# Writing out a layer loop, and moving norms, roundings and transfers ahead, in a two-block network on one core

## The chip, the core and the metric

The kernel runs on one core of a Trainium2 chip. The metric is the device time of one execution in microseconds (us). The core has five engines with queues of their own: PE (TensorE, matmuls), DVE (VectorE), ACT (ScalarE), POOL (GpSimd) and SP (SyncE, which here only starts transfers). They meet through semaphores alone.

## The reference

The input is x, 512 tokens of 1024 features. The first block has two layers. In short:

```
for l in range(2):
    hn = rms_norm(h, g_mix[l]); q, k, v, xr, gr = split(hn @ w_in[l])      # 2560 columns
    q, k = partial_rope(q), partial_rope(k)                                # angles from positions
    lam = exp(sum lam_q0*lam_k0) - exp(sum lam_q1*lam_k1) + lam_init
    o = rms_norm(diff_attention(q, k, v, lam)) * (1 - lam_init)
    y = rg_lru(conv(xr)) * gelu(gr)                                        # rates from softplus(-lru_lambda)
    h = h + concat(o, y) @ w_out[l]
    h = h + square(relu(rms_norm(h) @ w_mlp_in[l])) @ w_mlp_out[l]         # 4096 wide
    h = h + sigmoid(rms_norm(h) @ w_ple_gate[l]) * (p[l] @ w_ple_proj[l])
x = rms_norm(h, g_final)
```

The second block takes that x and a context of 256 tokens, together T = 768. Its first layer is a Mamba-like mixer in 8 head groups: a projection, a convolution, two scans (forwards and backwards), a gate by silu(z), an RMS norm over all 2048 inner features of a token, and an output product; the residual is `h + gate * out`. Its second layer is an attention over the 768 tokens, with 512 outputs, and a last RMS norm. Both layers take scale, shift and gate of every feature from silu(c) @ mod_w. Everything is float32.

## The kernel before

**Layout.** Activations stand with features on partitions: `h` is 128 partitions x 8 blocks x 512 tokens. A sum over features is therefore a matmul with a matrix of ones, and its result is the same row on all 128 partitions.

**Weights.** All large weights are a stream of tiles of 128x2048 floats (1 MB). SP fetches tile n into `wraw` (2 slots). POOL splits it into a rounded part `whi` and a rest `wlo` (2 slots): first four `tensor_scalar`, then four `tensor_tensor`. PE makes three matmuls of each product (whi*hi, wlo*hi, whi*lo), which keeps float32 accuracy. POOL begins tile n+2 when PE has ended tile n (`tile_done`), and PE begins a tile when all of it is split (`wsplit`). A layer has 52 tiles: 10 for `w_in` (`pair(j)`), 4 for `w_out`, 32 for the MLP, 1 for `w_ple_proj`, 4 for the gate and 1 of zeros, which makes the number even, so that the slot is `k % 2` in both passes of the loop. PE doesn't multiply the zero tile; SP fetches it and POOL splits it.

**Inputs of a product.** ACT rounds g*h to `uhi` (one instruction per block of 128 features), DVE writes the rest to `ulo`, PE's first tile of a product waits block by block for `ulo_r`. The norm's factor `rstd` is not in the input: it is applied by DVE when it reads PSUM (`mix_out`, L1544). ACT squares h two blocks at a time, DVE adds the squares into `acc2`, and `norm_sum` makes the sum by a matmul with ones; then come ACT's root and DVE's reciprocal.

**Layers.** `with pe.Fori(0, DEPTH) as l` and the same on ACT and DVE: one body in the program, run twice. At the end of a pass each engine reports, DVE clears all of the layer's semaphores and raises `layer_go`. Then ACT rounds and squares all eight blocks of the finished h for the next layer.

**Opening.** SP starts x and eight small transfers, and then the weights. ACT and DVE wait for all of them (`CST`). DVE makes the rotary angles (L1466 to L1473), ACT their sine and cosine and the tanh for silu(c), and PE waits for all that (`INIT_D`, `INIT_A`).

**Mixer of a layer.** DVE's order behind the first sum: reciprocal, the softplus chain for the LRU's rates (12 small instructions from L2222), `mix_out(0)`, `conv(0)`, `conv(1)`, `mix_out(1)`, `conv(2)`, `conv(3)`, `mix_out(2)`, `mix_out(3)`. ACT: two squares of `gr`, then eight tanhs of the gate products (L452 on PE, L1067 on ACT), which free two PSUM banks by turns.

**Behind the scan.** The last head group ends with eight output blocks on PE, each added by DVE to `oacc` (L1999). Then: `acc` (squares over the features) times ones, a root and a reciprocal over 768 columns (`rs2`); DVE's residual, three instructions per block (L2052, L2054); ACT's squares of it, two blocks at a time; the sum by 16 matmuls, root and reciprocal of 768 columns; and `make_in`, which makes the attention's input block by block (DVE `tin`, ACT scale and shift and `inhi`, DVE `inlo`). PE's first attention tile (K) waits for `inlo` block by block in its first half; its second half follows.

## Time and profile before

| | |
|---|---|
| median of 3 runs | 2680.79 us (2674.96 to 2684.66) |
| the profiled execution | 2680.21 us, span 2678.3 us, mean granted clock 0.965 |
| PE busy | 2442.2 us, 91% of the span |
| DVE, POOL, ACT busy | 54%, 49%, 30% |
| chain that ended last | PE 74%, DVE 15%, issue 5%, ACT 4% |
| HBM read | 194.60 MB, 75 GB/s over the span |

The span runs from the first to the last instruction on an engine. Busy is the time in which an engine has an instruction under way. The chain is followed back from the last instruction, at each step to what released it; its shares say which engines set the end.

### The profile page before, as it was taken

How to read it: one execution, taken by the hardware profiler on the slowest of the kernel's cores; microseconds unless marked ns; L12 is line 12 of the kernel's file. 1: busy time of each engine (PE TensorE's matmuls, PEld its weight loads, DVE VectorE, ACT ScalarE, POOL GpSimd, SP SyncE). 2: the span in 40 equal slices, each digit the busy share in tenths (PEclk: the TensorE clock that was granted, in tenths of full speed). 3: DMA queues.
4: the chain of work that ended last, by engine and by line, in shares of the span. 5: the costliest groups of instructions: out<-in, count | busy, mean ns of one | idle time of the engine just before them, and what ended most of it. 6: DMA issues, size and time to landing. Idle time of an engine off the chain costs nothing.

```text
span 2678.3 us, 36153 instructions
## 1 busy us (share of the span) xinstructions
PE 2442.2 (91%) x13200; PEld 2025.8 (76%) x13200; DVE 1444.3 (54%) x1780; ACT 798.8 (30%) x1700; POOL 1314.4 (49%) x1220
## 2 busy tenths in 40 slices
PE   5988999999797899999977799999999996798997
PEld 4656888888675688888855688988988885676876
DVE  7665311223575541121436787887888886326762
ACT  2224210112221520110214334333333332325771
POOL 5733766767676176766771243442444441153003
PEclk9989999999899999999998899999999997999999
DMA  4210344332222023343231011111110112021001
GB/s 144 73 60 32 110 140 135 126 134 94 96 79 79 17 102 129 131 142 134 90 129 63 32 48 47 46 42 37 47 47 31 60 34 89 16 88 54 2 1 47
DMA packets 33839, 201.44 MB, mean 75 GB/s; under 512 B 4416, under 2 KB 6592, under 8 KB 13632
## 3 DMA queue, kind: packets, MB, share of 16 engines
q1 hardware_dynamic: 23328, 164.13, 17.6%
q10 hardware_dynamic: 10400, 35.73, 4.2%
q8 instruction: 82, 1.34, 0.2%
q14 instruction: 29, 0.24, 0.0%
HBM read 194.60 MB, written 5.24 MB: 75 GB/s over the span
## 4 chain that ended last, share of the span: by engine, by line
PE 74%; DVE 15%; issue 5%; ACT 4%; POOL 1%; DMA 0%; ACTq 0%; DVEq 0%; SPq 0%; POOLq 0%
PE ps L385 40%; PE ps L628 11%; PE ps L850 5%; DVE convd L1810 3%; PE ps L746 2%; PE ps L605 1%; PE ps L724 1%; PE ps L763 1%; PE ps L493 1%; PE ps L408 1%; PE ps L931 1%; PE ps L948 1%; DVE convd L1824 1%; PE ps L572 1%; ACT tin L1192 1%
## 5 line engine op out<-in xcount | busy, mean ns | idle before, releaser
L337 POOL TENSOR_SCALAR whi<-wraw 128x512 fp32r<-128x512 f32 x608 | 412.8, 708 | 1339.6 <-PE ps L628 610.1
L341 POOL TENSOR_TENSOR wlo<-wraw,whi 128x512 fp32r<-128x512 f32 x608 | 907.4, 1524 | 0.0
L385 PE MATMUL ps<-uhi,whi 128*128 128x512 f32 x960 | 383.9, 400 | 49.4 <-DVE ulo L1499 40.6
L385 PE MATMUL ps<-uhi,wlo 128*128 128x512 f32 x960 | 377.2, 393 | 0.0
L385 PE MATMUL ps<-ulo,whi 128*128 128x512 f32 x960 | 376.3, 392 | 0.0
L628 PE MATMUL ps<-inhi,whi 128*128 128x384 f32 (+1 forms) x816 | 258.9, 354 | 45.3 <-DVE inlo L1754 28.3
L385 PEld LDWEIGHTS ps<-uhi,whi 128*128 128x128 f32 x960 | 182.0, 190 | 95.1 <-issue 48.2
L628 PE MATMUL ps<-inhi,wlo 128*128 128x384 f32 (+1 forms) x816 | 246.1, 338 | 0.0
L628 PE MATMUL ps<-inlo,whi 128*128 128x384 f32 (+1 forms) x816 | 245.8, 338 | 0.0
L1672 DVE TENSOR_TENSOR h<-h,ps 128x1024 f32<-128x1024 f32 x40 | 48.8, 1221 | 306.7 <-PE ps L385 306.7
L385 PEld LDWEIGHTS ps<-uhi,wlo 128*128 128x128 f32 x960 | 182.4, 190 | 38.8 <-issue 1.9
L385 PEld LDWEIGHTS ps<-ulo,whi 128*128 128x128 f32 x960 | 182.2, 190 | 38.7
L385 PE MATMUL ps<-hidhi,whi 128*128 128x512 f32 x512 | 202.2, 395 | 0.0
L385 PE MATMUL ps<-hidhi,wlo 128*128 128x512 f32 x512 | 199.5, 390 | 0.0
L385 PE MATMUL ps<-hidlo,whi 128*128 128x512 f32 x512 | 199.2, 389 | 0.0
L628 PEld LDWEIGHTS ps<-inhi,whi 128*128 128x128 f32 (+1 forms) x816 | 151.4, 190 | 55.4 <-issue 40.4
L628 PEld LDWEIGHTS ps<-inhi,wlo 128*128 128x128 f32 (+1 forms) x816 | 152.5, 190 | 2.4
L1284 ACT ACTIVATE ebuf<-ps,tabg 128x128 f32<-128x128 f32 x384 | 104.6, 384 | 164.4 <-PE ps L735 112.8
L1689 DVE SCALAR_TENSOR_TENSOR hm<-ps,rstd 128x1024 f32<-128x1024 f32 x32 | 39.2, 1224 | 211.8 <-PE ps L385 211.8
L628 PEld LDWEIGHTS ps<-inlo,whi 128*128 128x128 f32 (+1 forms) x816 | 151.7, 189 | 0.9
L1810 DVE SCALAR_TENSOR_TENSOR convd<-raw,cpg,convd 128x770 f32<-128x770 f32 x128 | 142.7, 1115 | 2.3
L1133 ACT ACTIVATE hsq<-hm 128x1024 f32<-128x1024 f32 x32 | 33.9, 1061 | 296.5 <-DVE hm L1689 296.5
(369 smaller groups left out, 4505.9 us busy)
## 6 DMA issues: line engine op xcount, KB each, us to landing
wraw<-in_wstream SPq DMA_DIRECT2D x152, 1024.0 KB, 4.9
modraw<-in_modw ACTq DMA_DIRECT2D x48, 512.0 KB, 3.6
hspill<-hres ACTq DMA_DIRECT2D x1, 3072.0 KB, 9.4
hback<-hspill ACTq DMA_DIRECT2D x1, 3072.0 KB, 10.8
h<-in_x SPq DMA_DIRECT2D x1, 2048.0 KB, 7.5
out<-hfin SPq DMA_DIRECT2D x2, 1024.0 KB, 4.0
gw<-in_gates ACTq DMA_DIRECT2D x2, 512.0 KB, 5.2
pT<-in_pT ACTq DMA_DIRECT2D x2, 512.0 KB, 6.0
```

Of the source, the lines that this page charges most:

```text
L337: pool.tensor_scalar(whi[:, s, c], wraw[:, s, c], 1.0, 0.0, ALU.mult, ALU.add).then_inc(wraw_read, 1)
L341: ins = pool.tensor_tensor(wlo[:, s, c], wraw[:, s, c], whi[:, s, c].bitcast(F32), ALU.subtract)
L385: mm = pe.matmul(ps[:, 2 * bank + m, :], a[:, w, c:c + P], b[:, kb, :], start=(n == 0 and i == 0), stop=(n == KB - 1 and i == 2))
L408: mm = pe.matmul(ps[32 * j:32 * j + 2, 5, 0:P], cvec[:, kb, :], modraw[:, kb, :], start=(half == 0), stop=(half == 1))
L628: mm = pe.matmul(ps[0:width, q + half, 0:HALF], a[:, s, c:c + width], b[:, kb, half * HALF:(half + 1) * HALF], start=(n == 0), stop=(n == ...
L746: mm = pe.matmul(ps[:, 6, d * 256:(d + 1) * 256], ck[:, c * P:(c + 1) * P], ast[:, slot, :], start=True, stop=True)
L850: mm = pe.matmul(ps[:, q + m, :], a[:, k % 2, c:c + P], b[:, kb, t0:t0 + S], start=(kb == 0 and i == 0), stop=(kb == KB - 1 and i == 2))
L1133: A(hsq[n % 2][:, :, :], hm[n % 2][:, :, :], ACT.Square).then_inc(L["sqh_r"], 1)
L1284: ins = A(ebuf[:, d, r, :], ps[:, 4 + d, r * P:(r + 1) * P], ACT.Exp, bias=tabg[:, K_NB + 2 * c + d, r:r + 1])
L1672: V.tensor_tensor(h[:, 2 * j:2 * j + 2, :], h[:, 2 * j:2 * j + 2, :], TWO(bank), ALU.add).then_inc(L["h_r"], 1)
L1689: V.scalar_tensor_tensor(out=hm[n % 2][:, :, :], in0=TWO(n % 2), scalar=0.0, in1=rstd2, op0=ALU.max, op1=ALU.mult).then_inc(L["m_r"], 1)
L1810: ins = V.scalar_tensor_tensor(out=o, in0=r[:, n:n + CW], scalar=cpg[:, 6 * b + n:6 * b + n + 1], in1=o, op0=ALU.mult, op1=ALU.add)
```

## The change

- **Layers written out.** The three loops over the layers become Python loops. Semaphores are no longer cleared: each wait adds `l * PER[name]`, the number of increments of a layer. The zero tile goes (51 tiles a layer), and the slot is `(l * LAYER_TILES + k) % 2`.
- **Between the layers.** PE's last gate tile runs block by block and reports each (`u_free`). ACT rounds (`next_rounded`) and squares the next layer's input, DVE writes the rests (`next_rest`), as far as h is ready, between the operations of the last gates. The softplus chain of layer 1 and its `gates` and `pT` transfers move into and behind the MLP of layer 0.
- **First sums.** `norm_sum(1)` and the product for lambda stand in the middle of tile 1, not between tiles 0 and 1.
- **Opening.** ACT starts x in two halves; SP starts the layers' parameters, tile 0, `misc`, tile 1, and then the other constants (`cst2`). POOL splits tiles 0 and 1 quarter by quarter, and PE follows (`w_piece`). PE's waits for the init go. DVE makes the softplus chain first; the angles stand behind `conv(3)` of layer 0, ACT's sine and cosine behind its first root and exp, the sign of `ropeS` behind `mix_out(7)`, silu(c) behind the second norm's reciprocal.
- **Behind the scan.** The sum of squares is made per token with tokens on partitions: 6 products of `acc`'s 128 columns with one column of ones give 128x6; root and reciprocal are of 6 columns, and `recip_rows` spreads them over the partitions by six products with the identity. It stands between output blocks 2 and 4; the residual of a block follows its last add. `hback` is fetched into the place of `inhi`, before the last group's output. The second norm is made the same way with one set of six products per block, and `make_in` reads its factor from PSUM. The K tile takes both halves per block.

The core of the diff, without the renamed waits:

```diff
-LAYER_TILES = MIX_TILES + 4 + 8 * CHUNKS + 1 + 4 + 1
+LAYER_TILES = MIX_TILES + 4 + 8 * CHUNKS + 1 + 4
...
+        sp.dma_start(lpall[:, :, :], io["lparams"]).then_inc(cst, 16)
+        sp.dma_start(wraw[:, 0, :], io["wstream"][0]).then_inc(wland[0], 16)
+        sp.dma_start(misc[:, :], io["consts"][:, 256:272]).then_inc(cst, 16)
+        sp.dma_start(wraw[:, 1, :], io["wstream"][1]).then_inc(wland[1], 16)
...
+        for s in range(2):
+            pool.wait_ge(wland[s], 16)
+            pool.wait_ge(tile_done, s + 1)
+            for n in range(PIECES):
+                c = slice(n * (TILE // PIECES), (n + 1) * (TILE // PIECES))
+                pool.tensor_scalar(whi[:, s, c], wraw[:, s, c], 1.0, 0.0, ALU.mult, ALU.add).then_inc(wraw_read, 1)
+                pool.wait_ge(wraw_read, s * PIECES + n + 1)
+                pool.tensor_tensor(wlo[:, s, c], wraw[:, s, c], whi[:, s, c].bitcast(F32), ALU.subtract
+                                   ).then_inc(w_piece, 1)
...
         # PE, in tile()
+                if midway and m == 0 and n == 4:
+                    midway()
...
+                if kfree and m == 1 and n < KB - 1:
+                    mm.then_inc(kfree, 1)
...
-            pe.wait_ge(tile_done, l * LAYER_TILES + (LAYER_TILES - 1 + CREDIT))
-            pe.sem_inc(tile_done, 1)
-            pe.sem_inc(L["layer_done"], 1)
-            pe.wait_ge(layer_go, l + 1)
...
+        def recip_rows(n):
+            pe.wait_ge(n_rs, n)
+            for c in range(NC):
+                mm = pe.matmul(ps[:, 6 + c // 3, c % 3 * P:(c % 3 + 1) * P], rcol[:, NC + c:NC + c + 1].broadcast_to([P, P]),
+                               ident[:, :], start=True, stop=True)
+            mm.then_inc(rb_ps, 1)
...
             for j in range(2, KB):
                 out_block(j)
+                if last and j == 2:
+                    pe.wait_ge(acc_r2, GROUPS + 1)
+                    for c in range(NC):
+                        mm = pe.matmul(ps[:, 6, 400 + c:401 + c], acc[:, c * P:(c + 1) * P], ones[:, 0:1],
+                                       start=True, stop=True)
+                    mm.then_inc(n_ss, 1)
+                if last and j == 3:
+                    recip_rows(3)
...
+        for j in range(KB):
+            pe.wait_ge(n_sq, 8 + j + 1)
+            for c in range(NC):
+                mm = pe.matmul(ps[:, 6, 420 + c:421 + c], sq4[:, j % 3, c * P:(c + 1) * P], ones[:, 0:1],
+                               start=(j == 0 and c == 0), stop=(j == KB - 1), skip_group_check=True)
+            mm.then_inc(n_ss, 1)
+        pe.wait_ge(n_x, 2 * KB)
+        recip_rows(4)
...
         # ACT
+        for j in range(2):
+            act.dma_start(h[:, 4 * j:4 * j + 4, :], io["x"][:, 4 * j:4 * j + 4, :]).then_inc(x_land[j], 16)
...
             A(small[:, 2:4], ps[:, 6, 0:2], ACT.Exp).then_inc(L["lam_r"], 1)
+            if l == 0:
+                rotary()
...
+                if j == 2 and l < DEPTH - 1:
+                    next_rounded(0)
+                    next_rounded(1)
+                    next_squared(0)
+                    next_squared(1)
+                    next_rounded(2)
+            if l < DEPTH - 1:
+                next_rounded(3)
+                next_squared(2)
+                next_squared(3)
...
         # DVE
             conv(2)
             conv(3)
+            if l == 0:
+                angles()
             mix_out(2)
             mix_out(3)
...
+                if j == 3 and l < DEPTH - 1:
+                    next_rest(4)
                 dve.wait_ge(L["gth_r"], l * PER["gth_r"] + j + 1)
...
+                if j == 2 and l < DEPTH - 1:
+                    for b in range(4):
+                        next_rest(b)
+            if l < DEPTH - 1:
+                for b in range(5, KB):
+                    next_rest(b)
...
+                for j in range(3):
+                    out_add(j)
+                token_recip(3)
+                dve.wait_ge(spill, 32)
+                dve.wait_ge(rr_r, 1)
                 for j in range(KB):
-                    out_add(j)
+                    if j >= 3:
+                        out_add(j)
+                    residual(j)
```

## Rows read from the trace of the kernel before

**Rows 1.** The page, part 1 (busy us, share, instructions) and part 6.

```profile
PE 2442.2 (91%) x13200; PEld 2025.8 (76%) x13200; DVE 1444.3 (54%) x1780; ACT 798.8 (30%) x1700; POOL 1314.4 (49%) x1220
...
h<-in_x SPq DMA_DIRECT2D x1, 2048.0 KB, 7.5
```

**Rows 2.** PE's waits, whole span: us in total, times, longest.

```profile
PE ps L385 <- DVE ulo L1499: 40.6, 2, 25.2
```

**Rows 3.** Timeline of the opening: start, us, instruction, idle before, releaser.

```profile
11.51 0.23 DVE L1463 CAST identb<-ident 128x128 bf16<-128x128 f32 x1 [10.50 <-DMA posi<-in_positions]
...
16.70 0.72 DVE L1473 TENSOR_SCALAR angt<-angt 128x512 f32<-128x512 f32 x1
...
24.17 10.39 DVE L1499 SCALAR_TENSOR_TENSOR ulo<-h,lp,uhi 128x512 fp32r<-128x512 f32 x8 [1.19 <-ACT uhi L1014]
...
25.22 0.76 PE L385 MATMUL ps<-uhi,whi 128*128 128x512 f32 x1 [25.22 <-DVE ulo L1499]
...
40.70 1.98 PE L395 MATMUL ps<-acc,ones 128*128 128x512 f32 x4 [2.01 <-DVE acc L1508]
```

**Rows 4.** Timeline of layer 0's first evictions and gates, DVE and ACT.

```profile
46.83 0.48 DVE L2222 TENSOR_SCALAR small<-small 128x4 f32<-128x4 f32 x1
...
50.45 1.23 DVE L1544 TENSOR_TENSOR proj<-ps,rstd 128x1024 f32<-128x1024 f32 x1
...
70.54 1.21 DVE L1544 TENSOR_TENSOR proj<-ps,rstd 128x1024 f32<-128x1024 f32 x1
...
77.85 1.25 ACT L1067 ACTIVATE ga<-ps,small 128x512 f32<-128x512 f32 x2
```

**Rows 5.** The chain in order of time: start, us, what.

```profile
42.80 32.81 PE ps L385 x144
...
84.37 21.82 PE ps L385 x96
...
2320.13 17.27 PE ps L832 x144
```

**Rows 6.** Timeline between the layers.

```profile
690.21 7.00 POOL L341 TENSOR_TENSOR wlo<-wraw,whi 128x512 fp32r<-128x512 f32 x4
...
691.37 2.20 DVE L1709 SCALAR_TENSOR_TENSOR h<-gth,h 128x1024 f32<-128x1024 f32 x1
...
702.30 2.17 DVE L1709 SCALAR_TENSOR_TENSOR h<-gth,h 128x1024 f32<-128x1024 f32 x1
...
713.90 0.77 PE L385 MATMUL ps<-uhi,whi 128*128 128x512 f32 x1 [15.35 <-DVE ulo L1499]
714.47 0.63 PE L385 MATMUL ps<-uhi,wlo 128*128 128x512 f32 x1
714.90 0.63 PE L385 MATMUL ps<-ulo,whi 128*128 128x512 f32 x1
...
727.57 1.88 PE L395 MATMUL ps<-acc,ones 128*128 128x512 f32 x4
```

**Rows 7.** Timeline of DVE behind the scan.

```profile
2246.74 0.95 DVE L1999 TENSOR_TENSOR oacc<-oacc,ps 128x768 f32<-128x768 f32 x1 [1.16 <-PE ps L628]
...
2264.61 0.99 DVE L2052 TENSOR_TENSOR oacc<-oacc,rs 128x768 f32<-128x768 f32 x1
...
2280.00 1.15 DVE L2054 SCALAR_TENSOR_TENSOR oacc<-oacc,modv,hback 128x256 f32<-128x256 f32 x2
...
2291.59 1.83 DVE L1759 TENSOR_TENSOR tin<-oacc,rs 128x768 f32<-128x768 f32 x2
...
2309.48 0.96 DVE L1754 TENSOR_TENSOR inlo<-tin,inhi 128x768 fp32r<-128x768 f32 x1 [1.12 <-ACT inhi L1196]
```

**Rows 8.** Timeline of DVE in the last head group, with and without POOL at work.

```profile
2207.62 1.75 DVE L1905 TENSOR_TENSOR ebuf<-ebuf 128x512 f32<-128x512 f32 x1
...
2216.33 0.69 DVE L1905 TENSOR_TENSOR ebuf<-ebuf 128x512 f32<-128x512 f32 x1
```

**Rows 9.** Timeline of PE, one turn of a modulation row in the MLP.

```profile
338.69 0.28 PE L419 MATMUL ps<-misc,modrow 128*128 128x2 f32 x2
```

More of the change, by code:

```diff
@@ L148, in build @@
     rtmp = at("rtmp", 192, [P, 2, S])
+    sqn = [at(f"sqn{i}", 136 + 4 * i, [P, 2, S]) for i in range(3)]
     sqmlp = at("sqmlp", 168, [P, 2, S])
@@ L986, in _ @@
         A = act.activation
+        for j in range(2):
+            act.dma_start(h[:, 4 * j:4 * j + 4, :], io["x"][:, 4 * j:4 * j + 4, :]).then_inc(x_land[j], 16)
         act.wait_ge(cst, CST)
-        A(small[:, 0:16], cvec[:, :, :].rearrange("p a b -> p (a b)"), ACT.Tanh, scale=0.5).then_inc(init_a, 1)
-        act.wait_ge(init_d, D_ANGLE)
-        A(ropeS[:, :], angt[0][:, :], ACT.Sin).then_inc(init_a, 1)
-        A(ropeC[:, :], angt[0][:, :], ACT.Abs).then_inc(init_a, 1)
-        act.wait_ge(init_a, 3)
@@ L994, in _, with rotary @@
-        A(ropeC[:, :], ropeC[:, :], ACT.Sin, scale=-1.0, bias=misc[:, 2:3]).then_inc(init_a, 1)
-        act.wait_ge(init_d, INIT_D)
-        with act.Fori(0, DEPTH) as l:
-            st = Chain(act, L["a_step"])
+        def rotary():
+            act.wait_ge(init_d, D_ANGLE)
+            A(ropeS[:, :], angt[0][:, :], ACT.Sin).then_inc(init_a, 1)
+            A(ropeC[:, :], angt[0][:, :], ACT.Abs).then_inc(init_a, 1)
+            act.wait_ge(init_a, 2)
+            A(ropeC[:, :], ropeC[:, :], ACT.Sin, scale=-1.0, bias=misc[:, 2:3]).then_inc(init_a, 1)
@@ L1298, in group @@
             z_tanh(1)
-            if not last:
+            if last:
+                act.dma_start(hback[:, :, :], hspill).then_inc(spill, 16)
+            else:
                 copy_in(s1, 0, blk0 + 2, None)
@@ L1327, in _ @@
         act.wait_ge(u_r, 2 * GROUPS)
-        act.wait_ge(sqz_r, GROUPS)
-        act.dma_start(hback[:, :, :], hspill).then_inc(spill, 16)
-        root(3, halves(rs2[:, :]), both, 1.0 / MDI)
-        act.wait_ge(n_rt, 3)
+        root(3, rcol[:, 0:NC], ps[:, 6, 400:400 + NC], 1.0 / MDI)
+        act.wait_ge(rb_ps, 1)
+        A(halves(rs2[:, :]), ps[:, 6:8, 0:HALF], ACT.Copy).then_inc(rr_r, 1)
         for dst, src in ((bones, io["consts2"][:, 512:640]), (perm2, io["consts2"][:, 640:768]),
@@ L1334, in _ @@
             act.dma_start(dst[:, :], src).then_inc(ld3, 16)
-        for j in range(4):
-            act.wait_ge(n_x, KB + 2 * j + 2)
-            A(sq4[:, 2 * j:2 * j + 2, :], oacc[:, 2 * j:2 * j + 2, :], ACT.Square).then_inc(n_sq, 1)
-        root(4, halves(rs2[:, :]), both, 1.0 / D)
+        for j in range(KB):
+            act.wait_ge(n_x, KB + j + 1)
+            if j >= 3:
+                act.wait_ge(n_ss, 3 + j - 2)
+            A(sq4[:, j % 3, :], oacc[:, j, :], ACT.Square).then_inc(n_sq, 1)
+        act.wait_ge(n_ss, 3 + KB)
+        A(rcol[:, 0:NC], ps[:, 6, 420:420 + NC], ACT.Sqrt, scale=1.0 / D, bias=misc[:, 0:1]).then_inc(n_rt, 1)
         make_in(1)
-        blk0 = 2 + 10 * (GROUPS - 1) + 8
+        done_wait(T_ATT)
         for m in range(2):
-            act.wait_ge(blk_ps, blk0 + 1) if m == 0 else done_wait(T_ATT)
             src = ps[:, 2 * m:2 * m + 2, 0:HALF]
@@ L1559, in _ @@
             lambdas()
-            dve.wait_ge(L["proj_r"], 1)
+            dve.wait_ge(L["proj_r"], l * PER["proj_r"] + 1)
             conv(0)
@@ L1855, in _, with token_recip, residual @@
         dve.wait_ge(spill, 16)
+        def token_recip(n):
+            dve.wait_ge(n_rt, n)
+            V.reciprocal(rcol[:, NC:2 * NC], rcol[:, 0:NC]).then_inc(n_rs, 1)
+        def residual(b):
+            dve.wait_ge(o_rd, 8 * GROUPS + b + 1)
+            st(V.tensor_tensor(oacc[:, b, :], oacc[:, b, :], rs2[:, :], ALU.mult))
+            for t0, t1, c in SEG:
+                ins = V.scalar_tensor_tensor(out=oacc[:, b, t0:t1], in0=oacc[:, b, t0:t1], scalar=modv[0][:, 16 + b, c:c + 1],
+                                             in1=hback[:, b, t0:t1], op0=ALU.mult, op1=ALU.add)
+            ins.then_inc(n_x, 1)
         def group(g, last):
```

508 lines of the change are left out of this document (274 added, 234 removed).

## The prediction

> **What bounds the kernel now.** I read the page first: PE is busy for 2442.2 us of the 2678.3 us span [rows 1]. So only the 236 us between the two in which PE stands still, or runs at the lower of its two clocks, can be won, and this change removes no matmul of weight. The second view is PE's list of waits [rows 2]. Its longest line lies at places that the diff touches: 40.6 us for `ulo` in two waits, 25.2 at the start and so 15.4 between the layers. The third view is the timeline around these places [rows 3, 4, 6, 7]. The reader should see three stretches where PE has nothing: 0 to 25.2, 698.5 to 713.9, and behind the scan a norm of two stages in front of the first `inlo`. Everything outside them I take as unchanged, and say below where I checked what is late next.
>
> **Part A, the opening.** Before, x and seven small transfers must land (11.5), DVE does the angles until 17.4, tanh and sines of ACT follow, and the first matmul starts at 25.22 [rows 3]. Tile 1 starts at 42.80, and three tiles (144 matmuls) take 32.81, so 10.94 each; tile 2 thus starts at 53.7 and tile 3 ends at 75.6 [rows 5].
> After: x goes out on ACT's queue, beside weights 0 on SP's. Before, the 2 MB of x took 7.5 from issue to landing [rows 1]; x's first half, the parameters and weight tile 0 are 2 MB too, so I let them land at 8.3, and the second halves at about 13 (15.8 at most, twice the 7.5). DVE then does the softplus chain, which now stands in front of the rounding: it took 46.83 to 50.45, 3.6, with POOL idle [rows 4]; POOL splits beside it now, so I take 4.6 and start it at 8.9. The first `ulo` is there at about 14.7, and DVE's eight take 10.4 as before [rows 3]. POOL delivers a quarter of a tile every 2.1 to 2.5 and is ahead of PE. Tile 0 ran from 25.22 to 38.7 (the sum's 40.70 less its wait of 2.01 [rows 3]) and stays as long, so 14.7 to 28.1. Tile 1, now with the norm sum in its middle (1.9, from [rows 6]), ends at 40.8, and the 2.0 wait for the sum of squares in front of it is gone. The root, the 3.4 reciprocal and the first eviction follow the sum at 35.2 and end at 40.65: just in time. Tile 2 starts at 40.8 in place of 53.7: 12.9 gained.
> Most of it is given back. DVE: from its first eviction (50.45) to its third (70.54) were 20.1 of convolutions [rows 4]; so from 39.4 they end at 59.5. Now `angles()` stands there, in front of `mix_out(2)`. It took 11.51 to 17.42, 5.9, with POOL mostly idle [rows 3]. POOL is splitting now, and DVE operations with two SBUF operands go from 0.69 to 1.75 beside it [rows 8], so 7.5 (between 5.9 and 11). That ends at 67. Behind it on DVE wait `mix_out(2)` and `(3)` (1.2 each, to 69.5); behind it on ACT is `rotary()`, three activations to 69, which has put itself in front of the squares of `gt` and the gate tanhs. ACT then does two squares and one load of the tanh table (it had none there before, since Sin was not the last function): first gate tanh ready at 73.4, against 78.5 before (the first of the two from 77.85 [rows 4]). PE ends tile 3 at 62.6, does two gate matmuls, and waits some 9 us for that tanh. After such a gap PE is on the low clock: behind the 15.35 gap its matmuls are 0.43 apart, not 0.227 [rows 6]. The six remaining gate products, 5.8 before, then take about 7.7. Tile 4 starts at 81.2 in place of 84.37 [rows 5]: 3.2 gained, not 12.9. The signs scaling of `ropeS` now sits between `mix_out(7)` and the rotations that PE waits for; one such scaling took 0.72 [rows 3]: 0.7 lost. The silu of c (two operations of 16 columns) lies in the 10.9 of a tile, behind the reciprocal, and costs nothing; without that cover it would be 0.6. **A: 2.5 gained**, between 1 lost (angles 11) and 12 gained (the whole angle work hidden).
> The Trainium skill (TensorE: Matmul & The Clock Gate, HAM oscillation) says the same of gaps: an idle PE falls to 1.2 GHz, and the next burst starts cold. By it the 9 us gap costs about 2 more, as the row of the 15.35 gap makes it; without it A would be 4.5.
>
> **Part B, between the layers.** Before, gate tile 3 ends at 698.5; DVE finishes h at 704.5, then come the hand-over of the loop, the rounding by ACT and `ulo` by DVE, and PE starts at 713.90, the first 13 matmuls at 0.43; the norm sum begins at 727.57 [rows 6]. POOL's split whose second half ran from 690.21 to 697.2 was of the zero tile.
> After: without the zero tile that split is of layer 1's tile 0 and is done at 697.2. Blocks 0 to 3 are rounded while gate tile 3 runs (`u_free` frees one every 1.36). ACT has them by 694; DVE can begin behind the update of h for j=2, 693.6 [rows 6], and needs 4 x 1.3, so 698.8. PE starts tile 0 at 698.6 and does a block in 1.36. Blocks 4, 5: DVE ends 4 at 701.3, in front of the last gate operations (its last h at 704.8), 5 at 706.1, then 6 and 7 at 707.4 and 708.7. Tile 0 ends at 710.2 in place of 727.57. The norm sum moves inside tile 1 and costs its 1.88 as before. The next dependences have more room than before: the split of tile 1 is done by 708, the sum of squares at 712.4 when PE asks at 712.9, and the softplus chain has gone from in front of the first eviction into the MLP, where DVE has one operation per 10.9 us tile. **B: 17.3 gained.** If blocks 4 to 7 come at 1.8 each (the slowest operation of the group that [rows 3] sum up as 10.39 for eight), 14; if POOL never disturbs DVE, 19. At the end of layer 1 only the hand-over goes, for which I count nothing.
>
> **Part C, behind the scan.** Before [rows 7]: behind the last output block come sum, root and a 768-column reciprocal, the first residual at 2264.61, the last one done at 2281.15, so 2.07 per block; the second norm until 2291.59; the last `inlo` done at 2310.44, 18.85 later. The K tile, whose second half ran only afterwards, is done at 2320.13 [rows 5].
> After: the sum of squares per token is six products of one column each behind output block 2. A full fp32 product of 128x128 weights on 2 columns is two instructions and takes 0.28, its tail included [rows 9]; six one behind another are at most 1.7, and I take 1.3 on the high clock and 2.6 on the low one. Root and reciprocal are of 6 columns, 0.2 each. PE spreads them in six products, 1.3, behind block 3, and ACT copies 0.9: `rs2` at about 2252.4 if output block 2 ends at 2246.7 as in this execution [rows 7]. hback comes 50 us before it is needed. DVE then has 8 residuals x 2.07 and 5 adds x 1.0, 21.5, to 2273.9; POOL's split of the next tile now lies on the last three of them (before it lay on the reciprocal), and by [rows 8] I add 3: 2276.9. Output blocks 6 and 7 wait for DVE's adds and end at 2265.2. The eight sums of `sq4` stand behind them on PE: 8 x 1.3 catch up with DVE, last one at about 2279.7 with one on the low clock. Root, reciprocal and spreading: `make_in` starts at 2282.4 in place of 2291.59, 9.2 gained. Its own pace is unchanged (it now reads the factor from PSUM; the eviction of 1024 columns from PSUM took 1.23 [rows 4], so 768 take 0.92, and two from SBUF took 1.83 [rows 7]), so the last `inlo` is at 2301.3. The K tile now takes both halves per block, 12 x 0.174 = 2.1, just DVE's pace; starting cold it lags by some 2. Done at about 2305.5. **C: 14.6 gained**, between 5 (all eight sums on the low clock: 8 x 2.6 from 2266 ends at 2287, and `make_in` at 2290) and 20 (no POOL disturbance, full clock).
> The Trainium skill (SBUF, Who interferes with whom) says that a DVE instruction with two SBUF inputs is blocked outright by a GpSimd instruction that reads SBUF. The rows agree in kind (0.69 against 1.75). By full blocking residuals 5 to 7 would stand still for the 7.3 of the split, and C would be 10.
>
> **Sum.** 2.5 + 17.3 + 14.6 = 34.4. The profiled execution took 2680.2 around its span of 2678.3, within 0.6 of the runs' median 2680.8, so the forecast is 2646.
>
> **Rivals.**
> 1. The angles are hidden. If the two adds of time I make for ACT and POOL fall away, PE's gap behind tile 3 closes and A is up to 12: 2637. For it: DVE had 3.9 of slack in front of 75.63. Against: the order of the instructions on ACT is fixed, and 5.9 is more than 3.9.
> 2. The small sums are slow. PE works little between 2258 and 2280, stays on the low clock and DVE waits: C is 5, time 2656. For it: behind a gap the clock is low [rows 6], and six small products per 2 to 3 us leave PE half idle. Against: a backlog of five blocks keeps it busy at first.
> The Trainium skill's rule on the clock gate (same section) would side with this rival.
> 3. The overlap of the layers is partial: DVE serves gates and roundings in one queue, and each late `ulo` holds PE on a stop-and-go tile at the low clock. B is 9 (blocks at 1.8 and a cold tile): 2654.
> 4. Slower than before: layers written out are new code where the loop ran the same twice. If each engine's fetch of unseen code stopped PE, it would need over 34.4 / 102 layer tiles = 0.34 per tile. Against: layer 0 ran unseen code already, and its tiles 1 to 3 follow each other at 10.94 with no gap [rows 5], as 48 x 0.227 = 10.9 demands. It decides from 0.34 per tile; at 0.5 the time would be 2697.
>
> **How the numbers follow.** Forecast 0.52; rival 1 0.18, rival 2 0.16, rival 3 0.11, rival 4 0.03. A measurement of this kernel tells 0.3% (8 us) from no change. All cases but the last are faster by more. The sum of the best bounds is 51 (2629), of the worst 18 (2662); they don't come together, so the range is 2632 to 2661. Faster 0.96, same 0.02, slower 0.02.
>
> **What would show it.** The first matmul near 14.7 (not 25.2), and a PE gap of 9 us in front of the gate products, with ACT's tanh as its releaser; between the layers no PE wait over 2 us and no matmul at 0.43; `make_in` 9 us closer behind the scan, and K done 15 closer. Wrong it would be if x lands much later than 8.3, if the gap of the gates is missing, or if PE's sums behind the scan end after DVE's last residual by more than 5.

## The result and the profile after

The kernel after takes 2664.16 us in the median (2656.38 to 2668.36), against 2680.79: a ratio of 0.9931 with a 95% interval of 0.9906 to 0.9955. It is faster by 16.6 us in the medians (0.7%), clear of the noise, where 34.8 was forecast; 2664.2 lies outside the range of 2632 to 2661. The profiled execution took 2656.6 around a span of 2654.8, 23.5 shorter than the span of before. Executions of this kernel stand near 2656 with a mean granted clock (the share of 2.4 GHz that TensorE was given) of 0.966 to 0.968 and at 2662 to 2668 with 0.962 to 0.965, and the profiled one is of the first kind. The ledger below therefore has a second column, from the trace of a control run of the same kernel (span 2660.2, 18.1 shorter).

PE's busy time hardly moves, as [rows 1] let one expect; the page's first part:

```profile
PE 2444.1 (92%) x13296; PEld 2036.5 (77%) x13296; DVE 1442.7 (54%) x1778; ACT 799.3 (30%) x1706; POOL 1299.8 (49%) x1204
```

The opening, from the timeline of the kernel after (start, us, instruction, idle before, releaser). It answers to [rows 3]:

```profile
11.20 0.21 ACT L1054 ACTIVATE small<-lpall 128x4 f32<-128x4 f32 x1 [8.24 <-DMA misc<-in_consts]
...
11.67 1.18 DVE L2354 TENSOR_SCALAR small<-small 128x4 f32<-128x4 f32 x1 [0.19 <-ACT small L1055]
12.88 0.18 DVE L2355 RECIPROCAL small<-small 128x4 f32<-128x4 f32 x1
...
13.49 1.26 POOL L337 TENSOR_TENSOR wlo<-wraw,whi 128x512 fp32r<-128x512 f32 x1
13.65 1.13 DVE L2358 TENSOR_SCALAR small<-small 128x4 f32<-128x4 f32 x1
14.72 0.62 POOL L335 TENSOR_SCALAR whi<-wraw 128x512 fp32r<-128x512 f32 x1
14.81 3.83 DVE L2360 SCALAR_TENSOR_TENSOR small<-small 128x4 f32<-128x4 f32 x6
...
22.34 0.76 PE L399 MATMUL ps<-uhi,whi 128*128 128x512 f32 x1 [22.34 <-DVE ulo L1597]
...
73.36 3.66 DVE L1556 SCALAR_TENSOR_TENSOR angt<-angt,angt 128x512 f32<-128x512 f32 x3
...
78.45 0.63 ACT L1034 ACTIVATE ropeS<-angt 128x512 f32<-128x512 f32 x1 [32.26 <-DVE angt L1558]
...
82.26 1.28 ACT L1131 ACT_TABLE_LOAD   x1
...
84.30 7.59 PE L474 MATMUL ps<-xc,gw 128*128 128x512 f32 x12 [11.10 <-ACT ga L1131]
```

The first product starts at 22.34. The reader should follow its cause upward: 17 operations on four or eight columns stand on DVE from 11.67 to 21.5, and they could not begin before 11.20, when the last 8 KB of parameters had landed. Further down, PE has done two of the eight gate products and then stands for 11.1 us, because ACT, whose tanh frees the PSUM bank, has itself been waiting for the angles on DVE, for 32.26 us. The first tanh came at 77.85 before [rows 4], here at 83.56, and the six products behind it start at 84.30. Tile 4 starts at 91.89 against 84.37 [rows 5].

Between the layers, DVE and PE, for [rows 6]:

```profile
699.23 5.85 DVE L1589 SCALAR_TENSOR_TENSOR ulo<-h,lpall,uhi 128x512 fp32r<-128x512 f32 x4
...
710.98 5.15 DVE L1589 SCALAR_TENSOR_TENSOR ulo<-h,lpall,uhi 128x512 fp32r<-128x512 f32 x3
...
712.78 0.50 PE L399 MATMUL ps<-uhi,whi 128*128 128x512 f32 x1 [1.67 <-DVE ulo L1589]
```

This 1.67 is the only wait that the timeline still shows in place of the 15.35: it lies in the middle of tile 0, in front of block 5, and its product takes 0.50, not 0.77. The second group of gate products of layer 1 starts at 755.42.

Behind the scan, for [rows 7]:

```profile
2238.64 0.96 DVE L1974 TENSOR_TENSOR oacc<-oacc,rs 128x768 f32<-128x768 f32 x1 [2.63 <-ACT rs L1409]
...
2245.81 1.01 PE L652 MATMUL ps<-uh,whi 128*128 128x384 f32 x2 [3.87 <-DVE oacc L2122]
...
2251.43 16.72 PE L845 MATMUL ps<-ones,sq 128*128 128x1 f32 x96
...
2257.55 3.05 DVE L1976 SCALAR_TENSOR_TENSOR oacc<-oacc,modv,hback 128x256 f32<-128x256 f32 x2
...
2262.58 1.15 DVE L1976 SCALAR_TENSOR_TENSOR oacc<-oacc,modv,hback 128x256 f32<-128x256 f32 x2
...
2268.89 2.90 PE L632 MATMUL ps<-ident,rcol 128*128 128x128 f32 x12 [0.74 <-DVE rcol L1969]
...
2271.83 1.82 DVE L1867 TENSOR_TENSOR tin<-oacc,ps 128x768 f32<-128x768 f32 x2 [3.08 <-PE ps L632]
```

The eight sums (96 instructions) are one block without a gap, and they end at 2268.15, 4.4 behind the last residual block (2263.73). The same stretch by windows (start and end, length, PE busy, instructions, granted clock, DMA's busy share, GB/s):

```profile
2250.00:2252.00 2.00, 2.00 (x16) 1.00 0.00 0
2252.00:2254.00 2.00, 2.00 (x20) 1.00 0.00 0
...
2256.00:2258.00 2.00, 2.00 (x11) 0.50 0.00 0
2262.00:2264.00 2.00, 2.00 (x11) 0.50 0.49 106
2266.00:2268.00 2.00, 2.00 (x11) 0.50 0.00 0
```

PE is busy for the whole of each window, and yet from 2256 on the clock stands at its lower level (1.2 of 2.4 GHz), and a window of 2 us holds 11 instructions where it held 20.

**The ledger.** The same landmarks in each trace, gain against the kernel before in us, forecast beside it (rounded, so that a sum may be off by 0.1):

| stretch | profiled run | control | forecast |
|---|---|---|---|
| A, to tile 4 of layer 0 (84.37 to 91.89) | -7.5 | -6.6 | +2.5 |
| rest of layer 0, to the last eviction of its MLP (642.43 to 648.18) | +1.8 | +2.1 | 0 |
| B, to the second group of gate products of layer 1 (765.35 to 755.42) | +15.7 | +15.6 | +17.3 |
| rest of layer 1 and block one, to PE's last product with the scan's offsets (2236.93 to 2223.14) | +3.9 | 0.0 | 0 |
| C, to the K tile's end (2320.13 to 2294.57) | +11.8 | +9.0 | +14.6 |
| behind it | -2.1 | -2.1 | 0 |
| sum | 23.5 | 18.1 | 34.4 |

### The profile page after: what moved, and what is told of

Read it like the earlier page. It is cut to its first block, busy times and chain, and to the rows that moved or that the text cites. A ratio compares the mean times of both kernels' runs of the same rounds, so it can differ in the third digit from the quotient of the medians.

```text
span 2654.8 us, 35777 instructions
## 1 busy us (share of the span) xinstructions
PE 2444.1 (92%) x13296; PEld 2036.5 (77%) x13296; DVE 1442.7 (54%) x1778; ACT 799.3 (30%) x1706; POOL 1299.8 (49%) x1204
## 4 chain that ended last, share of the span: by engine, by line
PE 74%; DVE 16%; issue 5%; ACT 3%; POOL 1%; DMA 0%; DVEq 0%; ACTq 0%; SPq 0%; POOLq 0%
PE ps L399 39%; PE ps L652 11%; PE ps L889 5%; DVE convd L1919 3%; PE ps L770 2%; PE ps L748 1%; PE ps L621 1%; PE ps L787 1%; PE ps L970 1%; PE ps L424 1%; PE ps L987 1%; DVE convd L1933 1%; PE ps L595 1%; PE ps L516 1%; PE ps L757 1%
## 5 line engine op out<-in xcount | busy, mean ns | idle before, releaser
L351 POOL TENSOR_SCALAR whi<-wraw 128x512 fp32r<-128x512 f32 x592 | 404.7, 711 | 1319.2 <-PE ps L652 569.7
L355 POOL TENSOR_TENSOR wlo<-wraw,whi 128x512 fp32r<-128x512 f32 x592 | 883.1, 1521 | 0.0
L399 PE MATMUL ps<-uhi,whi 128*128 128x512 f32 x960 | 383.0, 399 | 33.9 <-DVE ulo L1597 22.3
L652 PE MATMUL ps<-inhi,whi 128*128 128x384 f32 (+1 forms) x784 | 249.7, 353 | 30.9 <-ACT raw L1288 17.0
L652 PE MATMUL ps<-inhi,wlo 128*128 128x384 f32 (+1 forms) x784 | 237.7, 338 | 0.0
L652 PE MATMUL ps<-inlo,whi 128*128 128x384 f32 (+1 forms) x784 | 237.1, 337 | 0.0
L652 PEld LDWEIGHTS ps<-inhi,whi 128*128 128x128 f32 (+1 forms) x784 | 145.9, 190 | 38.4 <-issue 29.4
L652 PEld LDWEIGHTS ps<-inhi,wlo 128*128 128x128 f32 (+1 forms) x784 | 146.4, 190 | 2.5
L652 PEld LDWEIGHTS ps<-inlo,whi 128*128 128x128 f32 (+1 forms) x784 | 145.6, 189 | 1.0
```

The costliest lines, as they stand in the source:

```text
L351: pool.tensor_scalar(whi[:, s, c], wraw[:, s, c], 1.0, 0.0, ALU.mult, ALU.add).then_inc(wraw_read, 1)
L355: ins = pool.tensor_tensor(wlo[:, s, c], wraw[:, s, c], whi[:, s, c].bitcast(F32), ALU.subtract)
L399: mm = pe.matmul(ps[:, 2 * bank + m, :], a[:, w, c:c + P], b[:, kb, :], start=(n == 0 and i == 0), stop=(n == KB - 1 and i == 2))
L652: mm = pe.matmul(ps[0:width, q + half, 0:HALF], a[:, s, c:c + width], b[:, kb, half * HALF:(half + 1) * HALF], start=(n == 0), stop=(n == ...
```

## The experiments

Each is the kernel after with one edit, unless it says more; the code lines shown are abridged. Each was timed against the kernel before, so ratios are to before. Theories 1, 2 and 3 are those of the expectation above each result. The kernel after itself was 0.9931, and 0.9942 as a control run.

**Control.**

> The kernel after itself, unchanged, on the chip on which the next three run, so that they can be set against it. If the difference that was measured first (16.6 us in the medians, 23.5 in the profiled runs) is one of the kernels, the ratio to the kernel before is again between 0.991 and 0.9955. If it was luck of the runs, the ratio comes out under 0.990 or over 0.997.

Measured: 2663.13 us, ratio 0.9942 [0.9921 to 0.9963]. The difference is one of the kernels. The profiled execution is another one than that of the result (span 2660.2), and the sums behind the scan look worse in it:

```profile
2248.20 1.01 PE L652 MATMUL ps<-uh,whi 128*128 128x384 f32 x2 [3.88 <-DVE oacc L2122]
...
2255.22 18.30 PE L845 MATMUL ps<-ones,sq 128*128 128x1 f32 x96
...
2263.03 3.05 DVE L1976 SCALAR_TENSOR_TENSOR oacc<-oacc,modv,hback 128x256 f32<-128x256 f32 x2
...
2274.26 2.90 PE L632 MATMUL ps<-ident,rcol 128*128 128x128 f32 x12 [0.74 <-DVE rcol L1969]
```

They end at 2273.5, 7.4 behind the last residual block (2266.1).

**The opening of before in the kernel after.** Fetch order, init work, unsplit pieces, softplus behind the norm, sums between tiles 0 and 1.

```
+ init work of ACT, DVE in front; pe.wait_ge(init_d, INIT_D); pe.wait_ge(init_a, INIT_A)
- angles() in front of mix_out(2); rotary() in front of the squares of gt
- pieces of tiles 0 and 1, x on ACT's queue
```

> The opening of the kernel before (fetch order, all initial work in front of TensorE, tile 0 and 1 split whole, angles first, decay rates behind the norm, first sums between tiles 0 and 1); everything behind the opening as in the kernel after. Theory 1 (the new opening as a whole loses): tile 4 of layer 0 starts again near 84.4 us instead of 91.9, and the kernel is about 7 us faster than the kernel after, near 2657 against its 2664. Theory 2 (the later start of tile 4 is given back by the rotary stage and the attention, which begin with less to wait for): the gap closes before the end of the layer, and the time is that of the kernel after within 2 us. Theory 3 (the new opening gains, as the prediction had it, and the loss is elsewhere): 3 us slower than the kernel after.

Measured: 2654.9 us, ratio 0.9911 [0.9889 to 0.9933], 5 to 8 us faster than the kernel after by the ratios. Tile 4 starts at 82.17, 9.7 earlier. Theory 1: the new opening as a whole loses. The intervals overlap, so the sign rests on the trace as well, and there it is plain: the product of the lambdas, behind the norm sum in tile 1 of layer 1, is at 715.04 against 722.10 (720.88 in the control). This product serves as the landmark of the next three runs too. Behind it this execution gives some back: the first product of block one is at 1419.76, against 1420.66 in the kernel after and 1423.00 in the control.

**Angles late.**

```
-            if l == 0:
-                angles()
             mix_out(2)
...
+            if l == 0: angles_first()      # six operations
             mix_out(4)
...
+            if l == 0: angles_rest()       # four operations
             mix_out(5)
# ACT: rotary() behind the Sqrt of gt; posi, maskf, angt at 128 to 134 KB
```

> The kernel after with the ten VectorE operations of the angles moved out of the stretch in front of the third mixer output: six stand behind the gate's last product, in front of mix_out(4), four in front of mix_out(5), and the sines on ScalarE behind the square root of the gate. Theory 1 (the angles are what TensorE waits for in front of the gate's products): the wait of 11.1 us there shrinks to about 3, gate products at 76, tile 4 near 83 to 84, and 8 to 9 us faster than the kernel after. Theory 2 (the angles only move: mix_out(4) and mix_out(5) come late and hold tiles 6 and 7 back): tile 4 starts at 83 but tile 7 ends where it ended, and nothing is gained. Theory 3 (the wait there is set by the convolutions, not by the angles): less than 2 us gained.

Measured: 2647.2 us, ratio 0.9890 [0.9867 to 0.9914], 11 to 14 us faster than the kernel after. Its timeline:

```profile
74.98 5.80 PE L474 MATMUL ps<-xc,gw 128*128 128x512 f32 x12 [1.26 <-ACT ga L1129]
...
90.32 0.43 DVE L1554 TENSOR_SCALAR angt<-angt 128x512 f32<-128x512 f32 x1
91.81 1.22 DVE L1641 TENSOR_TENSOR proj<-ps,rstd 128x1024 f32<-128x1024 f32 x1 [1.06 <-PE ps L399]
...
95.17 3.82 DVE L1559 SCALAR_TENSOR_TENSOR angt<-angt,angt 128x512 f32<-128x512 f32 x3
...
102.69 1.22 DVE L1641 TENSOR_TENSOR proj<-ps,rstd 128x1024 f32<-128x1024 f32 x1 [2.26 <-PE ps L399]
```

The wait of 11.10 is 1.26, and the products are back at 5.80: the gap and the low clock behind it went together. Theory 2 fails on the rows at 91.81 and 102.69: DVE stood idle for 1.06 and 2.26 in front of them although operations of the angles had just run there. The angles are hidden in these two places. The landmark in layer 1 is at 712.64, 9.5 earlier (8.2 against the control).

**Constants in front of the first weights.**

```
         sp.dma_start(lpall[:, :, :], io["lparams"]).then_inc(cst, 16)
+        sp.dma_start(misc[:, :], io["consts"][:, 256:272]).then_inc(cst, 16)
         sp.dma_start(wraw[:, 0, :], io["wstream"][0]).then_inc(wland[0], 16)
-        sp.dma_start(misc[:, :], io["consts"][:, 256:272]).then_inc(cst, 16)
```

> The kernel after with the 8 KB of constants (the misc columns) fetched in front of the first weight tile instead of behind it: the first small operation of ScalarE, which waited until 11.2 us, can begin near 3 to 4 us. Theory 1 (the late parameters and the softplus chain beside the GpSimd split are why the first product waited until 22.3 us): the chain of 21 small operations takes some 3.6 us in place of 9.8, ends before the split begins, and the first product starts near 13 to 15 us, where the prediction had it; the whole comes 5 to 8 us forward, and the kernel is that much faster. Theory 2 (the first product is set by x and the rests on VectorE beside the split anyway): the first product at 18 or later and under 3 us gained.

Measured: 2658.03 us, ratio 0.9923 [0.9901 to 0.9946], 2 to 5 us faster than the kernel after; not to be told from it by times alone. The timeline of this kernel is clear:

```profile
6.76 0.21 ACT L1054 ACTIVATE small<-lpall 128x4 f32<-128x4 f32 x1 [3.79 <-DMA misc<-in_consts]
...
8.25 1.15 DVE L2360 SCALAR_TENSOR_TENSOR small<-small 128x4 f32<-128x4 f32 x6
...
13.46 0.80 PE L399 MATMUL ps<-uhi,whi 128*128 128x512 f32 x1 [13.46 <-POOL wlo L337]
...
76.30 7.33 PE L474 MATMUL ps<-xc,gw 128*128 128x512 f32 x12 [11.17 <-ACT ga L1131]
```

The parameters came at 6.8, not at 3 to 4. The six operations take 1.15, not 3.83; the whole chain (17 operations, not the 21 of the expectation) takes 3.4 and is over at 10.6, before POOL's first split begins at 11.07. The first product starts at 13.46; the prediction had 14.7. Now POOL's first piece releases it. The gap in front of the gates stays at 11.17, and the landmark in layer 1 is 8.6 earlier than in the kernel after (713.54). The first product of block one (1415.70 against 1420.66) is only 5.0 earlier: 3.6 go in layer 1, where between 700 and 900 us the mean granted clock is 0.94 here and 0.97 in the profiled run of the kernel after. The control, with 0.94, shows that the profiled run is the exception: against it this kernel is 7.3 earlier at both places (713.54 against 720.88, 1415.70 against 1423.00).

**Both edits.**

> Both edits: constants in front of the first weight tile, and the angles late. If each does what its first theory says, tile 4 of layer 0 starts near 76 us instead of 91.9, and the kernel is 13 to 16 us faster than the kernel after, near 2650 in the median. If one hides behind the other, it is as fast as the better of the two alone, about 8 us faster than the kernel after.

Measured: 2639.63 us, ratio 0.9851 [0.9830 to 0.9873], 21 to 24 us faster than the kernel after, more than forecast. The gate products start at 65.58 with a wait of 1.26, 18.7 earlier, and the landmark in layer 1 at 701.38, 20.7 earlier (19.5 against the control): the two add up, 8.6 and 9.5, and bring 2.6 more.

**The step between the layers as before.** The layers stay written out, fetches and softplus stay early.

```
-                     kfree=L["u_free"] if j == 3 and l < DEPTH - 1 else None)
- next_rounded / next_squared behind gate tile 2; next_rest(b) between the gates
+            else:
+                act.wait_ge(tile_done, l * LAYER_TILES + CREDIT)
+                act.wait_ge(L["h_r"], l * PER["h_r"])
+                (roundings, squares; rests on DVE)
```

> The kernel after with the step from layer 0 to layer 1 as in the kernel before: the rounding, the squares and the rests of layer 1 begin only when all of layer 0's gate tiles and its new h are done; the layers stay written out and the fetches of the gates' weights stay early. Theory 1 (the overlap of the two layers brings what the two traces show, 15.7 us between the last gate tile and tile 4 of layer 1): 14 to 16 us slower than the kernel after. Theory 2 (a good part of the 15.7 us is not the overlap but the end of the loop: copy of the parameters, clearing of the semaphores, fetches): 9 to 12 us slower. Theory 3 (what is gained there is given back in the attention of layer 1, where the clock falls): under 6 us slower.

Measured: 2671.19 us, ratio 0.9967 [0.9951 to 0.9983], 7 to 10 us slower than the kernel after.

```profile
716.26 3.17 ACT L1072 ACTIVATE uhi<-h,lpall 128x512 fp32r<-128x512 f32 x5 [3.58 <-DVE h L1810]
717.99 0.76 PE L399 MATMUL ps<-uhi,whi 128*128 128x512 f32 x1 [7.66 <-DVE ulo L1594]
```

PE waits 7.66, not 15.35. From the last eviction of layer 0's MLP to the second group of gate products of layer 1 it is 122.9 in the kernel before (642.43 to 765.35), 114.1 here (654.20 to 768.25) and 107.2 in the kernel after (648.18 to 755.42). So of B's 15.7 the overlap is worth 6.8, and 8.9 come without it: theory 2 in kind, and with 6.8 below its bound by the traces. Of the 8.9, 7.7 are the shorter wait, which is the end of the loop; 1.2 lie behind the first product, where this kernel also has the norm's sum in the middle of tile 1 and no softplus chain. What each of these two is worth was not tried. In the kernel before, the first rounding came 6.8 behind the last h (704.47 to 711.29): the hand-over, the copy of the parameters and a load of ACT's table stood there. Here it comes 0.1 behind it.

**The part behind the scan as before.**

```
- sums per token, recip_rows(3) between output blocks; residual(b) behind out_add(b)
+ norm over 128x768 behind the last output block; hback at 120 KB; squares in four steps; K tile in two halves
```

> The kernel after with the part behind the scan as in the kernel before: one sum over all columns behind the last output block, residual blocks one after the other behind it, squares in four steps, reciprocal over 128x768, and the K tile in two halves. Theory 1 (what the two traces say: this part brought 11.7 us): 11 to 13 us slower than the kernel after, the K tile done near 2306 in place of 2294.6. Theory 2 (the prediction's sum for this part): 14.6 us slower. Theory 3 (the part only moved waiting, and the rest comes from somewhere else): less than 5 us slower.

Measured: 2672.27 us, ratio 0.9982 [0.9967 to 0.9996], 11 to 14 us slower than the kernel after: theory 1. From the last turned pair of the scan to the end of the K tile it takes 82.7 (2226.70 to 2309.35), 83.4 in the kernel before, 71.6 in the profiled run of the kernel after and 74.4 in the control: 8 to 11 by the traces, where the times say 11 to 14.

**Added products that keep PE working.**

```
+        def warm(n):
+            for _ in range(n):
+                pe.matmul(ps[:, 0, 0:P], ones[:, :], ident[:, :], start=True, stop=True)
# 12 in front of sum 6, 6 in front of sum 7, 3 in front of recip_rows(4), 16 behind it
```

> The kernel after with products of ones and the identity, 128x128 each and read by nobody, put into TensorE's idle time behind the scan: 12 in front of the sums of the seventh square, 6 in front of the eighth, 3 in front of the second spreading of the reciprocals and 16 behind it. Theory 1 (the small sums and the spreading are slow because the clock has fallen while TensorE waited, and this is what the last part of the prediction missed): the last six sums take 1.3 us in place of 3.5, the spreading 1.5 in place of 2.9, the first products of the K tile run at their high spacing, and the kernel is 4 to 6 us faster than the kernel after. Theory 2 (these small products are limited by something else, or the clock doesn't rise in so short a time): the rows stay, and the kernel is up to 3 us slower, by what the added products hold back.

Measured: 2657.61 us, ratio 0.9932 [0.9911 to 0.9954], the same as the kernel after.

```profile
2256.69 13.13 PE L850 MATMUL ps<-ones,sq 128*128 128x1 f32 x72
2269.68 4.39 PE L843 MATMUL ps<-ident,ones 128*128 128x128 f32 x24
2273.91 1.40 PE L850 MATMUL ps<-ones,sq 128*128 128x1 f32 x12
...
2278.64 1.60 PE L632 MATMUL ps<-ident,rcol 128*128 128x128 f32 x12
...
2284.59 0.94 PE L866 MATMUL ps<-inhi,whi 128*128 128x384 f32 x4 [0.77 <-DVE inlo L1869]
```

Both theories are half right. Under the added 128-column products the clock rises to its upper level (0.50 from 2260 to 2272, 1.00 from 2274 on): one square's sum takes 1.40 where the six before averaged 2.2, the spreading 1.60 and not 2.90, and the K tile begins at full pace. But the added products waited in the same queue as the sums and cost 4.4 where they stood: the stretch is 74.1 long. A clock bought with work on the path was no gain here.

**The V tile's split late.**

```
+        for s in range(2):
+            if s == (T_ATT + 1) % 2:
+                pool.wait_ge(n_x, 2 * KB)
+            split(late, s)
```

> The kernel after with GpSimd's split of the V tile (the second behind the scan) held back until the last residual block is done; it is needed only at 2294. Theory 1 (the split slows VectorE's operations beside it: residual blocks five and six took 2.9 and 4.5 us for their multiply and their two fused operations where the others took 2.0): these blocks fall to 2.0 us each, the last residual block ends 3.5 us earlier, and the kernel is 3 to 3.5 us faster than the kernel after. Theory 2 (the split meets make_in instead and costs the same there): the first blocks of make_in grow by what is saved, and nothing is gained. Theory 3 (the later split makes the V tile wait): a wait for wlo in front of the V products, and slower.

Measured: 2662.06 us, ratio 0.9939 [0.9920 to 0.9957], no gain. None of the three theories holds for the time. The residual blocks do speed up, as theory 1 has it: eight of them and their adds take 21.5, from 2250.66 to 2272.11, against 25.1 in the kernel after, and nothing meets the split later. But

```profile
2263.44 16.73 PE L856 MATMUL ps<-ones,sq 128*128 128x1 f32 x96
```

the sums take their 16.7 whatever DVE does, and the stretch stays at 71.6. They end at 2280.17, 8.1 behind the last residual block: so they, not the residual blocks, end last.

**Three sums between the output blocks.**

```
+                if last and j == 6:
+                    square_sum(0); square_sum(1)
+                if last and j == 7:
+                    square_sum(2)
                 out_block(j)
```

> The kernel after with the sums of the first two squares behind the scan in front of the seventh output block and the third in front of the eighth, in place of all eight behind the last output block. In the control run the eight stand back to back from 2255.2 to 2273.5 on TensorE, at the low clock, and end 9 us after the last residual block. Theory 1 (the eight sums are what ends last there): three of them go into the 3.9 us in which TensorE waits in front of the seventh block, which also holds the clock longer; five are left behind the last block, the last ends 3 to 6 us earlier, and the kernel is 3 to 6 us faster than the kernel after. Theory 2 (the residual blocks on VectorE end last): output block seven comes later by up to 2 us, and the kernel is the same or 1 us slower.

Measured: 2658.34 us, ratio 0.9923 [0.9904 to 0.9941], 2 to 5 us faster than the kernel after by the ratios and within both intervals. The wait of 3.9 in front of output block 6 is filled (0.54 left). Now PE waits for the last squares, and its sum is as slow as ever:

```profile
2268.45 3.04 DVE L1985 SCALAR_TENSOR_TENSOR oacc<-oacc,modv,hback 128x256 f32<-128x256 f32 x2
...
2272.41 2.72 PE L632 MATMUL ps<-ones,sq 128*128 128x1 f32 x12 [2.31 <-ACT sq L1426]
```

The stretch is 71.5 long: better than the control's 74.4, equal to the other run's 71.6. Two chains of nearly one length run here, and to shorten one alone shows little.

**The same with added products** (3, 6, 3, 3 and 14 of them).

> As the last, with added products of ones and the identity (128x128, read by nobody): 3, 6 and 3 in front of the sums of the sixth, seventh and eighth square, 3 in front of the second spreading, 14 behind it. Theory 1 (with the sums off the back, what is left is the low clock of the last sums, of the spreading and of the first products of the K tile): the spreading takes 1.5 us in place of 2.9, the K tile begins at its high spacing, and the kernel is 3 to 4 us faster than the last one. Theory 2 (the added products are themselves in the way, as in the run with them alone): no faster than the last one.

Measured: 2663.02 us, ratio 0.9936 [0.9916 to 0.9955]; the stretch is 72.7. Theory 2.

**All that helped, with late split and added products.**

> Constants in front of the first weight tile, angles late, sums between the output blocks, added products, and the V tile's split held back until the last residual block. The first two brought 21 us in ratio; with 3 to 6 us from behind the scan and 2 to 3 from residual blocks that are no longer beside the split, 24 to 30 us faster than the kernel after: ratio to the kernel before near 0.984. If the parts behind the scan bring nothing, it is 0.986.

Measured: 2634.12 us (2631.88 to 2637.79), ratio 0.9831 [0.9811 to 0.9850]. It beats both kernels, the one before by 47.7 us in the medians and the one after by 27 to 30 by the ratios. Nearly all of it comes from the first two edits; against them alone (0.9851) the intervals overlap, and the trace gives 1.2 us behind the scan (70.3 against 71.5).

## Why the prediction was wrong

**Part A is the step that failed**: it misses by 10.0 in the profiled run and by 9.1 in the control, more than any other part, and within it above all one term does: "The first `ulo` is there at about 14.7". PE's first product came at 22.3, and everything in the opening is later by that. Two things made up the 7.6. The parameters were to land at 8.3, with x's first half and tile 0, and DVE was to start at 8.9; but the last 8 KB of them stand behind a weight tile of 1 MB in SP's queue, came at 11.2, and DVE started at 11.67. Put in front of the tile, they came at 6.8. And the softplus chain was priced at 4.6, a quarter above its 3.6 "with POOL idle". It took 9.8. By the timeline the late start is 2.8 of the 7.6 and the chain 5.2, less 0.4 that the first `ulo` saved; no run parts the two, since early parameters remove both.

A share of its own time is the wrong form for this price, for what it pays is a wait. Ten of the 17 operations took longer than alone, and each of the ten began while POOL had an instruction under way and ended when that did, within 0.03: up to 1.18 beside a subtraction of the split (1.27, as the pair at 13.49 and 13.65 shows), 0.32 to 0.55 beside a multiplication (0.62), by how late they began in it. Six others took 0.16 or 0.17 and began between two of POOL's instructions; only the reciprocal ran at its 0.18 beside one. The sign stood in the rows of before: POOL was not idle there, its split ended at 47.29, and the chain's first operation in [rows 4] took 0.48, from 46.83 to 47.31, where the next of its form took 0.17. (The part on the kernel before counts 12 instructions in this chain; these are rows, and one stands for six.) The Trainium skill (SBUF — State Buffer, Who interferes with whom) has this form of it: the port pair that VectorE and GpSimd share is an exclusive lock, and whoever issues first has it for the whole instruction. This trace agrees: the ends coincide. The prediction cited the section for the residual blocks and did not carry it to the short operations.

A second term was 3.4 short. The 20.1 of convolutions from the first eviction to the third were moved forward as they stood, but the splits did not move with them. From the first eviction (46.83) to the angles (70.29) it is 23.5, for the most part since the first two convolutions now lie beside a split (48.60 to 58.52), the second one wholly beside its subtractions:

```profile
49.54 3.00 DVE L1646 SCALAR_TENSOR_TENSOR xc<-proj,lpall,xc 128x511 f32<-128x511 f32 x3
...
54.01 5.06 DVE L1646 SCALAR_TENSOR_TENSOR xc<-proj,lpall,xc 128x511 f32<-128x511 f32 x3
```

The same three operations took 2.56 and 3.69 in the kernel before, and the one in front of each went from 0.55 to 0.96 and from 0.84 to 1.51. The two terms make 11.0, and tile 4 came 10.7 after its forecast (91.89 against 81.2). The rest of A was right: the angles took 8.1 (7.5 forecast), PE's gap was 11.1 (9), the products behind it 7.6 (7.7), with ACT's tanh as the releaser. That this gap eats the gain was foreseen; with the late start it turned a gain of 2.5 into a loss of 7.5. The runs confirm both halves one by one: early parameters bring the landmark in layer 1 forward by 8.6, late angles by 9.5, both by 20.7. With both, the median is 2639.6, below the forecast of 2646.

**Part B** was 1.6 too large. The order of events was as told, down to one wait under 2 us. What the prediction did not have is its make-up: over half (8.9 of 15.7) comes without the overlap, 7.7 of it from the removed end of the loop.

**Part C** was 2.8 too large in the profiled run and 5.6 in the control: a size in the right chain. Moved to the same end of output block 2, `rs2` was ready when forecast (first residual 2252.4), and the last residual within 0.6. Then "The eight sums of `sq4` stand behind them on PE: 8 x 1.3 catch up with DVE" failed: eight times 1.3 was the upper clock's price, and they cost 2.1 to 2.3 each, with the spreading at 2.9, not 1.3. `make_in` gained 6.0 and not 9.2 (3.0 in the control). So rival 2 described the mechanism, and of its price of 9.6 (14.6 less 5) 2.8 were paid in one execution and 5.6 in the other. The prediction's own sign, sums that end more than 5 behind the last residual, is absent in the first (4.4) and there in the second (7.4). The ground that rival 2 gave was another one, though: PE half idle. By the profile PE always had a product under way, and the clock fell while one-column products followed each other. How much of that time the array multiplied is not shown.

**Left over**: the medians gained 16.6, the profiled pair 23.5, the control's trace 18.1. The 3.9 of "rest of layer 1" are luck of the profiled execution: from the second gate products of layer 1 to the first product of block one it took 665.2, and the control 668.8, like the runs with early constants, with both edits, with the part behind the scan as before, and with all edits (668.8 to 669.2). The granted clock between 700 and 900 us goes with it: 0.97 against 0.94 in the control, 0.97 also with late angles (665.4), 0.93 with the opening of before (671.4). The other 2.8 between the two lie in C, where the output blocks 6 and 7 (7.2 against 5.8) and the sums (18.3 against 16.7) met more of the lower clock. What decides which of them an execution gets was not tried. Two terms that the prediction put at nothing are the same in both traces, +2 in the rest of layer 0 and -2.1 behind the K tile; they cancel, and their cause was not looked for.

## What to carry to other kernels

Price small VectorE operations beside GpSimd per instruction, by what is left of GpSimd's instruction, and not as a share of their own time: here a chain of 17 took 3.4 in front of the first split and 9.8 beside it. Read each queue in order before you let a small transfer land early. Work that is moved "into a wait" has to be laid against the wait's own end: the same ten operations cost 9.5 us in front of one eviction and nothing that the trace shows in front of two later ones.

## What the runs showed of the hardware

- Low clock with PE busy: from 2258 to 2272 of the control, one-column fp32 products followed each other without a gap in the profile, and the granted clock was 0.50 throughout. It had been 0.95 and 0.90 in the four us before, under 384-column products and the first sums.

```profile
2254.00:2256.00 2.00, 2.00 (x16) 0.95 0.00 0
2256.00:2258.00 2.00, 2.00 (x18) 0.90 0.00 0
2258.00:2260.00 2.00, 2.00 (x11) 0.50 0.03 8
2262.00:2264.00 2.00, 2.00 (x12) 0.50 0.00 0
```

- Six sums over one column are twelve instructions, 1.40 at the upper level and about 2.2 in a row at the lower; spreading six columns over 128, 1.50 and 2.90.
- VectorE operations of 128x4 took 0.16 to 0.18 alone. Begun while POOL split a tile, ten of 17 ended together with POOL's instruction (1.12 to 1.18 beside one of 1.27, 0.32 to 0.55 beside one of 0.62); the reciprocal did not wait.
- POOL pays too: four multiplies of a split took 3.66 beside VectorE and 2.37 without it.
- 8 KB behind 1 MB in one queue landed 4.4 us later than in front of it.
